# RMS norms of a two-block transformer kernel: another way to sum the squares and to make the inverse root

## The reference, cut to what matters

```python
def rms_norm(x, g):
    x32 = x.astype(jnp.float32)
    y = x32 * lax.rsqrt(jnp.mean(x32 * x32, axis=-1, keepdims=True) + EPS)
    return (y * g.astype(jnp.float32)).astype(x.dtype)

# first block
h = rms_norm(x, g_pre_mix[l]) * (1.0 + sc1) + sh1
merged = concatenate([rms_norm(y_a, g_out_sgu[l]), rms_norm(y_b, g_out_attn[l])], axis=-1)
x = x + g1 * rms_norm(o, g_post_mix[l])
h2 = rms_norm(x, g_pre_ffn[l]) * (1.0 + sc2) + sh2
x = x + g2 * rms_norm(f, g_post_ffn[l])
# second block
xn = rmsnorm(x, norm1_g[l])
x = x + sq_relu_mlp(rmsnorm(x, norm2_g[l]), w_up, w_down)
return rmsnorm(x, norm_f_g)
```

## Time and profile before

| | |
|---|---|
| median of 3 runs | 4016.05 us (4013.57 to 4019.14) |
| the profiled execution | 4012.63 us, span 4010.9 us |
| mean granted clock of TensorE | 0.903 |
| TensorE matmuls busy | 3137.9 us (78%) |
| VectorE busy | 2441.0 us (61%) |
| ScalarE busy | 664.8 us (17%) |
| GpSimd busy | 314.4 us (8%) |
| reciprocals of the norms, L538 | 8 of 6.55 us |

### The profile page before, as it was taken

One profiled execution on the slowest core, in us unless ns is written; L12 is line 12 of the kernel. 1 busy time (PEld: TensorE's weight loads), 2 busy tenths in 40 slices (PEclk: granted clock), 3 DMA queues, 4 the chain that ended last, 5 costly groups with the idle time before them and its releaser, 6 DMA issues. The chain is left out here.

```text
span 4010.9 us, 46974 instructions
## 1 busy us (share of the span) xinstructions
PE 3137.9 (78%) x18184; PEld 2317.1 (58%) x18184; DVE 2441.0 (61%) x3161; ACT 664.8 (17%) x1134; POOL 314.4 (8%) x286
## 2 busy tenths in 40 slices
PE   2687608694999999949539977588887879999995
PEld 2564504372878787728318865233345668778784
DVE  5638996627456546673564654678765364664566
ACT  0203304311100010011323311222221111001000
POOL 0000010001000000010001100255520100000001
PEclk9898859897999999979759988799988889999998
DMA  8010000010222222221141111000122123223231
GB/s 317 24 41 16 32 0 1 36 49 24 97 89 95 89 96 90 93 91 48 55 153 42 62 62 58 11 21 11 42 87 81 42 63 95 89 89 95 89 99 73
DMA packets 97670, 275.34 MB, mean 69 GB/s; under 512 B 10864, under 2 KB 39664, under 8 KB 95856
## 3 DMA queue, kind: packets, MB, share of 16 engines
q1 hardware_dynamic: 97520, 273.24, 20.4%
HBM read 241.72 MB, written 31.49 MB: 68 GB/s over the span
## 5 line engine op out<-in xcount | busy, mean ns | idle before, releaser
L193 DVE CAST weight_high<-weight_ring 128x1024 fp32r<-128x1024 f32 (+1 forms) x324 | 217.3, 671 | 460.1 <-PE psum L301 207.4
L301 PE MATMUL psum<-h_half_high,weight_high 128*128 128x512 f32 x1024 | 404.3, 395 | 58.4 <-DVE h_half_low L195 54.4
L1356 PE MATMUL psum<-hidden_high,weight_high 128*128 128x512 f32 x1024 | 402.5, 393 | 23.7 <-DVE hidden_low L195 23.7
L301 PE MATMUL psum<-h_half_low,weight_high 128*128 128x512 f32 x1024 | 402.0, 393 | 0.0
L301 PE MATMUL psum<-h_half_high,weight_low 128*128 128x512 f32 x1024 | 401.7, 392 | 0.0
L1356 PE MATMUL psum<-hidden_low,weight_high 128*128 128x512 f32 x1024 | 401.4, 392 | 0.0
L1356 PE MATMUL psum<-hidden_high,weight_low 128*128 128x512 f32 x1024 | 401.2, 392 | 0.0
L195 DVE TENSOR_TENSOR weight_low<-weight_ring,weight_high 128x1024 fp32r<-128x1024 f32 (+1 forms) x324 | 384.3, 1186 | 11.2
L1288 DVE TENSOR_TENSOR hidden<-hidden (+1 forms) x128 | 88.6, 693 | 369.6 <-ACT hidden L1291 369.5
L2464 PE MATMUL psum<-h_again,weight_ring 128*128 128x512 f32 x512 | 238.0, 626 | 36.2 <-ACT gates L2590 36.2
L301 PEld LDWEIGHTS psum<-h_half_high,weight_high 128*128 128x128 f32 x1024 | 194.3, 190 | 105.9 <-issue 56.8
(11 more groups left out here) (434 smaller groups left out, 5165.5 us busy)
## 6 DMA issues: line engine op xcount, KB each, us to landing
weight_ring<-in_w_ff SPq DMA_DIRECT2D x128, 512.0 KB, 3.4
weight_ring<-in_w_ff_up SPq DMA_DIRECT2D x64, 512.0 KB, 3.5
weight_ring<-in_w_ff_down SPq DMA_DIRECT2D x64, 512.0 KB, 3.5
weight_ring<-in_w_ada SPq DMA_DIRECT2D x48, 512.0 KB, 5.1
h_again<-rwkv_parts SPq DMA_DIRECT2D x8, 1792.0 KB, 8.3
rwkv_parts<-parts SPq DMA_DIRECT2D x24, 512.0 KB, 5.5
weight_ring<-in_w_out SPq DMA_DIRECT2D x16, 512.0 KB, 3.5
x<-x SPq DMA_DIRECT2D x2, 4096.0 KB, 11.6
```

Source lines behind the costliest of these rows:

```text
L193: dve.tensor_copy(high, x).then_inc(sem, 1)
L301: mm = pe.matmul(psum[:, 2 * (j % 2) + h, 0:n], w, x(g * kt + k, lo, n), start=(g == 0 and k == 0 and m == 0), stop=(g == kg - 1 and k == ...
L1356: mm = pe.matmul(K.psum[:, g * OUTS + t, :], w[:, s % 2, at], x[:, s % 2, kk, :], start=(first and kk == 0 and m == 0), stop=(last and kk ...
```

## The change

The products of the norm change their operands: 128 tokens of the squares are the weight operand and one column of ones is the moving operand, so the sum of a pair lands with tokens on partitions, one column of PSUM bank 4 for each pair and each 128 tokens. VectorE adds the pairs' columns up and applies the mean and epsilon on 128 x 8 values. GpSimd raises them to the power of minus one half. VectorE multiplies the identity matrix by each of the 8 columns, which gives eight diagonal matrices in two halves; TensorE multiplies them by the matrix of ones, which puts the inverse root of every token on every partition, in PSUM banks 6 and 7. The scaling reads it there. The square root, the reciprocal and the tile `root` are gone. The diff, without the declarations of the new semaphores and their counts:

```diff
+        mean = K.sbuf(ctx, "mean_square", [P, NT])
+        power = K.sbuf(ctx, "minus_half", [P, NT])
+        diagonal = K.sbuf(ctx, "root_diagonal", [P, NT, P])
+        halves = NT // 2
...
-                act.wait_ge(K.sq_used.sem, used0 + pairs)
-                act.activation(root[:], K.psum[:, 4:6, :], ACT.Sqrt, scale=1.0 / size, bias=K.col(eps)) \
-                    .then_inc(K.root_ready.sem, 1)
...
                 for p in range(pairs):
                     pe.wait_ge(K.pair_summed.sem, pair0 + p + 1)
-                    for h in range(2):
-                        mm = pe.matmul(K.psum[:, 4 + h, :], K.const("ones"),
-                                       sq[:, p % 2, h * HALF:(h + 1) * HALF],
-                                       start=(p == 0), stop=(p == pairs - 1))
+                    for n in range(NT):
+                        mm = pe.matmul(K.psum[:, 4, p * NT + n:p * NT + n + 1], sq[:, p % 2, n * P:(n + 1) * P],
+                                       K.const("ones")[:, 0:1], start=True, stop=True)
                     mm.then_inc(K.sq_used.sem, 1)
+                for h in range(2):
+                    pe.wait_ge(K.diagonal_ready.sem, diagonal0 + h + 1)
+                    pe.matmul(K.psum[:, 6 + h, :], K.const("ones"),
+                              diagonal[:, h * halves:(h + 1) * halves, :].rearrange("p n t -> p (n t)"),
+                              start=True, stop=True).then_inc(K.scale_ready.sem, 1)
...
+                dve.wait_ge(K.sq_used.sem, used0 + pairs)
+                dve.tensor_reduce(out=mean[:], in_=K.psum[:, 4, 0:pairs * NT].rearrange("q (p n) -> q n p", p=pairs),
+                                  op=ALU.add, axis=AX.X).then_inc(K.total_ready.sem, 1)
+                dve.wait_ge(K.total_ready.sem, total0 + 1)
+                dve.tensor_scalar(mean[:], mean[:], 1.0 / size, EPS, op0=ALU.mult, op1=ALU.add) \
+                    .then_inc(K.mean_ready.sem, 1)
                 dve.wait_ge(K.root_ready.sem, root0 + 1)
-                dve.reciprocal(root[:], root[:]).then_inc(K.scale_ready.sem, 1)
-                dve.wait_ge(K.scale_ready.sem, scale0 + 1)
+                for h in range(2):
+                    some = slice(h * halves, (h + 1) * halves)
+                    dve.tensor_tensor(out=diagonal[:, some, :],
+                                      in0=K.const("ident").unsqueeze(1).broadcast_to([P, halves, P]),
+                                      in1=mean[:, some].unsqueeze(2).broadcast_to([P, halves, P]), op=ALU.mult) \
+                        .then_inc(K.diagonal_ready.sem, 1)
+                dve.wait_ge(K.scale_ready.sem, scale0 + 2)
                 for t in range(tiles):
                     to = src if add is not None else out
-                    dve.scalar_tensor_tensor(out=to[:, t, :], in0=src[:, t, :], scalar=gain(t), in1=root[:],
+                    dve.scalar_tensor_tensor(out=to[:, t, :].rearrange("p (h s) -> p h s", h=2), in0=src[:, t, :].rearrange("p (h s) -> p h s", h=2), scalar=gain(t), in1=K.psum[:, 6:8, :],
                                              op0=ALU.mult, op1=ALU.mult).then_inc(K.scaled.sem, 1)
...
-            if add is not None:
-                @block.gpsimd
-                def _(pool):
+            @block.gpsimd
+            def _(pool):
+                pool.memset(power[:], -0.5).then_inc(K.power_set.sem, 1)
+                pool.wait_ge(K.power_set.sem, power0 + 1)
+                pool.wait_ge(K.mean_ready.sem, mean0 + 1)
+                pool.tensor_tensor(out=mean[:], in0=mean[:], in1=power[:], op=ALU.pow)                     .then_inc(K.root_ready.sem, 1)
+                if add is not None:
                     for t in range(1, tiles, 2):
```

More of the change, by code:

```diff
@@ L114, in __init__ @@
         self.scale_ready = self.flag("scale_ready")
+        self.mean_ready = self.flag("mean_ready")
+        self.diagonal_ready = self.flag("diagonal_ready")
+        self.total_ready = self.flag("total_ready")
+        self.power_set = self.flag("norm_power_set")
         self.scaled = self.flag("scaled")
@@ L475, in rms_norm @@
         odd = K.sbuf(ctx, "odd_squares", [P, S])
-        root = K.sbuf(ctx, "root", [P, S])
+        mean = K.sbuf(ctx, "mean_square", [P, NT])
+        power = K.sbuf(ctx, "minus_half", [P, NT])
+        diagonal = K.sbuf(ctx, "root_diagonal", [P, NT, P])
+        halves = NT // 2
         pairs = tiles // 2
         odd0, pair0 = K.odd_ready.n, K.pair_summed.n
+        mean0, total0, diagonal0, power0 = K.mean_ready.n, K.total_ready.n, K.diagonal_ready.n, K.power_set.n
         sq0, used0, root0, scale0, scaled0 = (K.sq_ready.n, K.sq_used.n, K.root_ready.n,
@@ L559, in rms_norm @@
     K.root_ready.n += 1
-    K.scale_ready.n += 1
+    K.mean_ready.n += 1
+    K.power_set.n += 1
+    K.total_ready.n += 1
+    K.diagonal_ready.n += 2
+    K.scale_ready.n += 2
     K.scaled.n += tiles
```

## The result

The changed kernel takes 4029.8 us (median of 10 runs, 4022.34 to 4033.76); beside it the kernel before took 4016.5 (10 runs). The ratio is 1.0032 (95% interval 1.0022 to 1.0042): slower by 13 us, where 9.5 had been forecast. The profiled execution took 4024.44 us with a span of 4022.4; the one of the kernel before, 4012.63, lies at the low end of what that kernel shows.

A forecast was written before the change was run, and what follows sets the result against it. TensorE is busy 78% of the span, but each norm stands alone as a chain that is all span. Seven norms +15.4, the short norm -0.1, additions -5.8 gave +9.5, 4026 us; own range 4012 to 4042, 8 in 10 within 4002 to 4050.

The forecast's parts named there:

- The level of the clock, the deciding step: Sums of squares in the norms: TensorE stays at 1.2 GHz for all new pairs, each holding it for 3.43 us.
- six bursts of the same form: Modulation stage of the old trace: 96 one-column records whose weight loads took 287 to 339 ns, the low clock level.
- a run of 128 columns: Spatial mixing in the old trace: 16 records of 128 columns at clock 0.50, followed by 46 records at 1.00.
- rival A: Norms: the clock rises during the first pairs, later pairs take 2.0 us, total 3986 us; chance 0.16.
- T: Start of a norm's first odd square, from which its chain to the first scaling is timed; 21.00 us in the old last norm.
- A pair's products: Sums of squares on TensorE: pairs start 3.43 us apart, the last signal at T + 16.56.
- The power: GpSimd's power of 128x8 in each norm: 1.5 us taken, between 0.55 (per instruction) and 4.4 (per column).
- Diagonal and spreading product: After the power: first half diagonal on VectorE 0.69 us, then TensorE's ones product of both halves 3.82 us at the low level.
- The chain as a whole: T to first scaling: 23.2 us against 21.0, +15.4 in seven norms; short norm 16.34 against 16.47, -0.1.
- The additions: Two norms with an addition: the PSUM operand lets GpSimd run beside VectorE, 0.97 us saved three times in each, -5.8 us.
- Rival C: Two norms with an addition: no relief, as the in-place SBUF operand still shuts GpSimd out; +5.8, 4032 us; chance 0.10.
- The sum: Whole kernel: +15.4 - 0.1 - 5.8 = +9.5 us, from 4016.05 to 4026 us, +0.24%.

The follow-up runs named there:

- run with 128 columns: Changed kernel with all 128 columns of ones moving in the sums of squares instead of one: 3999.9 us, ratio 0.9952 to the kernel before.
- the run with this part alone: Kernel before with only its reciprocal written into PSUM and the scalings reading it there: 4013.0 us, ratio 0.9987.
- extra products: Kernel before plus unread one-column TensorE products behind the last pair of every norm: 4019.5 us, ratio 1.0004; only in the last two norms: 4017.1 us, 0.9998.
- the power in halves: Changed kernel with GpSimd's power made in two halves of 4 columns, each half diagonal waiting for its own: 4024.4 us, ratio 1.0016; with 128 moving columns too, 3990.2 us, 0.9933.

## Why the prediction was right, and where it was off

- **The level of the clock, the deciding step.** Forecast: 1.2 GHz for all pairs, on the evidence of six bursts of the same form against a run of 128 columns. Measured: the low level in all norms but the first 1.0 and 0.3 us of the pairs of two of them. The run with 128 columns shows that here the columns make the difference: it has the same loads. This is rival A's condition brought about by one edit. Its price was too high: 18.0 from T and -24.6 us in the norms were forecast, 17.7 to 20.0 and -15 to -16 measured, and 3999.9 where 3986 was forecast. The sums came out as A had them (last signal at T + 13.27 in the last norm, 13.15 forecast); the spreading product, priced at 2.0 throughout, ran at the low level in four of eight norms. Some 3 us more lie outside the norms.
- **A pair's products.** Forecast 3.43 apart, last signal at T + 16.56. Measured 64 records in 13.81 us and the reduce at T + 16.39.
- **The power.** 1.5 taken between 0.55 and 4.4, measured 1.646: 1.2 us in all. The truth is a mixture of a price per instruction and a price per column; that the middle of so wide a range lay this near it is luck in part. The Trainium skill, "GPSIMD Engine Reference", section "3.1 Elementwise — side-by-side cycle accounting", states some 2.6 cycles per element for an addition with two inputs, by which eight columns would come to an estimate of 0.57 us. That price does not carry over to the power: its columns cost 0.157 us each here.
- **Diagonal and spreading product.** 0.69 and 3.82 forecast, 0.70 and 3.80 measured.
- **The chain as a whole.** +15.3 forecast over the eight norms, +13.9 between the two first profiles (177.4 less 163.5), +14.6 against the repeats of the kernel before. The two norms that follow dense products began with a high clock and took 22.33 and 22.96; I had taken the low level for all. That the last norm hit 23.19 on 23.2 is two small errors that cancel: the last signal came 0.17 us earlier than forecast, and the power took 0.15 longer.
- **The additions.** -5.8 forecast, -5.8 measured, and -5.0 of time in the run with this part alone. Rival C is gone.
- **The sum.** +9.5 forecast, +8.1 to 8.8 in the norms, +13.3 and +10.5 in the medians. The rest of 2 to 5 us lies outside the norms. The interval of the ratio reaches down to 1.0019 to 1.0022, 7.6 to 8.8 us, so a rest of nothing is just within it. The chunk stage is 2.9 us longer on average with new norms, in ranges that overlap, and its long executions are those with the lower granted clock; extra products did not bring it about in the medians. What brings the clock down there stays open. The forecast had nothing for the time outside the norms.

## What to carry to other kernels

A chain that replaces one slow operation (6.55 us of reciprocal) by five short ones on three engines must be priced with the waits and with TensorE at 1.2 GHz; here the sums became the bound at the same moment. Before giving TensorE thin products, look in the trace for the same form and read its load times: the 334 ns there told the level of the clock, and with it the largest term. Where loads set the pace anyway, try wider moving operands: here 128 equal columns instead of one took no longer at the low level, the clock rose, and a loss of 13 us became a gain of 18, and together with the power in halves of 27. And where a stage outside the change seems to have moved, repeat the profile of the kernel before: here that stage alone varied by 6 us.

## What the runs showed of the hardware that was not expected

- With f32 loads of 128x128 alternating with products, moving operands of 1 and of 64 columns left the granted clock at 0.50 for 13 us of unbroken occupation; 128 columns were followed by 1.00. That 64 would match a single column so closely (13.91 against 13.81 us for 64 records) was new.
- GpSimd's power costs 0.39 us and 0.157 us per column of 128 values (0.548, 1.012 and 1.646 us for 1, 4 and 8 columns).
- A stage with many small products varied between 286.6 and 292.5 us in four executions with the same instructions in it and before it. In the longest the granted clock was 0.94 and the same matmuls were busy 260.2 us, in the shortest 0.96 and 256.4.
